# Delta stage with two inversions half a period apart, mask on VectorE, first operand space moved by 128 bytes, identity products at the stage's beginning

## The reference, cut to what matters

```python
m = jnp.where(strict, jnp.einsum('bhncd,bhnsd->bhncs', k_beta, k) * decay, 0.0)
t_inv = lax.linalg.triangular_solve(eye + m, ...)      # inverse of a 64x64 unit lower triangle
u = t_inv @ (v * beta);  w = t_inv @ (k_beta * exp(g))
def step(state, inp):                                  # 16 chunks, one after the other
    v_new = u_i - w_i @ state
    o = (q_i * exp(g_i)) @ state + a_i @ v_new
    state = state * exp(g_last) + k_dec.T @ v_new
# window: scores + mask (0 or -1e30) ; mx = max(max(scores), sink) ; p = exp(scores - mx) ; p @ v / denom
```

## Time and profile before

| | us |
|---|---|
| median of 3 runs | 2195.47 (2194.89 to 2196.8) |
| the profiled execution: its own time | 2197.01 |
| its span, first to last instruction | 2195.2 |
| delta_and_window, first GpSimd instruction to the next stage's | 335.89 to 717.39 |
| TensorE busy / VectorE / ScalarE / GpSimd | 2104.6 / 1120.2 / 725.2 / 353.0 |

### The profile page before, as it was taken

One profiled execution on the slowest core, in us unless ns is written; L12 is line 12 of the kernel. 1 busy time (PEld: TensorE's weight loads), 2 busy tenths in 40 slices (PEclk: granted clock), 3 DMA queues, 4 the chain that ended last, 5 costly groups with the idle time before them and its releaser, 6 DMA issues. The chain is left out here.

```text
span 2195.2 us, 33712 instructions
## 1 busy us (share of the span) xinstructions
PE 2104.6 (96%) x14274; PEld 1637.5 (75%) x14290; DVE 1120.2 (51%) x1724; ACT 725.2 (33%) x1344; POOL 353.0 (16%) x291
## 2 busy tenths in 40 slices
PE   7999997899998899999998999999999999999998
PEld 6888885567676687887775667778888888878877
DVE  6773335766756666563533664464433443442443
ACT  4113313333344334132314773452212212221221
POOL 3000003321322543021210323430000000000000
PEclk9999997999989899999999999999999999999999
DMA  6112322000000847712123103211111111111112
GB/s 217 48 48 86 96 87 92 1 2 2 2 2 2 302 139 275 266 40 58 59 78 150 52 17 135 77 58 48 39 58 48 38 57 51 43 39 53 49 34 101
DMA packets 186890, 167.40 MB, mean 76 GB/s; under 512 B 13472, under 2 KB 163828, under 8 KB 186100
## 3 DMA queue, kind: packets, MB, share of 16 engines
q1 hardware_dynamic: 180974, 146.75, 21.1%
q0 software_dynamic: 4784, 17.83, 2.1%
q10 hardware_dynamic: 982, 0.65, 0.1%
HBM read 138.48 MB, written 26.74 MB: 75 GB/s over the span
## 5 line engine op out<-in xcount | busy, mean ns | idle before, releaser
L250 PE MATMUL mix_acc<-mix_hi,w_hi 128*128 128x512 f32 x1040 | 415.0, 399 | 0.0
L252 PE MATMUL mix_acc<-mix_hi,w_lo 128*128 128x512 f32 x1040 | 409.3, 394 | 0.0
L251 PE MATMUL mix_acc<-m_lo,w_hi 128*128 128x512 f32 x1040 | 408.8, 393 | 0.0
L230 ACT ACTIVATE w_hi<-w_stage 128x1024 fp32r<-128x1024 f32 x154 | 162.6, 1056 | 463.3 <-PE mix_acc L252 247.2
L3178 DVE SCALAR_TENSOR_TENSOR hidden<-mix_acc,hidden_conv,hidden 128x1023 f32<-128x1023 f32 x88 | 112.8, 1282 | 263.5 <-ACT hidden L3127 262.0
L238 DVE TENSOR_TENSOR w_lo<-w_stage,w_hi 128x1024 fp32r<-128x1024 f32 x154 | 192.9, 1252 | 106.3 <-ACT w_hi L230 106.3
L250 PEld LDWEIGHTS mix_acc<-mix_hi,w_hi 128*128 128x128 f32 x1040 | 195.3, 188 | 52.0 <-issue 8.2
L252 PEld LDWEIGHTS mix_acc<-mix_hi,w_lo 128*128 128x128 f32 x1040 | 195.3, 188 | 45.7
L251 PEld LDWEIGHTS mix_acc<-m_lo,w_hi 128*128 128x128 f32 x1040 | 195.5, 188 | 43.4
L250 PE MATMUL acc<-h_hi,w_hi 128*128 128x512 f32 x400 | 156.8, 392 | 0.9 <-issue 0.9
L252 PE MATMUL acc<-h_hi,w_lo 128*128 128x512 f32 x400 | 155.8, 390 | 0.0
(11 more groups left out here) (365 smaller groups left out, 3644.0 us busy)
## 6 DMA issues: line engine op xcount, KB each, us to landing
w_stage<-in_w_in SPq DMA_DIRECT2D x48, 512.0 KB, 3.9
w_stage<-in_w_up SPq DMA_DIRECT2D x44, 512.0 KB, 3.7
w_stage<-in_w_out SPq DMA_DIRECT2D x32, 512.0 KB, 4.1
w_ada<-in_w_ada SPq DMA_DIRECT2D x32, 512.0 KB, 5.1
spill<-y_tok POOLq DMA_DIRECT2D x21, 512.0 KB, 5.1
m_resid<-resid_spill SPq DMA_DIRECT2D x2, 4096.0 KB, 16.9
conv_in<-in_w_ada SPq DMA_DIRECT2D x16, 512.0 KB, 5.6
w_stage<-in_w_down SPq DMA_DIRECT2D x16, 384.0 KB, 3.3
```

The lines of the kernel that those rows point to most:

```text
L230: nc.scalar.activation(w_hi[:, slot], w_stage[:, slot], ACT.Copy).then_inc(w_hi_ready, 1)
L250: nc.tensor.matmul(acc[:, h, :], w_hi[:, slot, k, :], hi[:, k, tok], start=k == 0, stop=False)
L251: nc.tensor.matmul(acc[:, h, :], w_hi[:, slot, k, :], lo[:, k, tok], start=False, stop=False)
L252: mm = nc.tensor.matmul(acc[:, h, :], w_lo[:, slot, k, :], hi[:, k, tok], start=False, stop=k == kts - 1)
```

## The change

1. The inversions of two steps run at once, half a period apart. A period has ten slots; the inversion of step s does levels 1 and 2 in period s (slots 1, 3, 5, 7) and levels 3 to 5 in period s+1 (slots 0, 2, 4, 6, 8, 9). The state part of step n is done in period n+2. There are 18 periods instead of 17. `tri` gets two banks; `kb` and `vb` become one bank, `value_bank`; the decays use `kvb1`. `pair_keys` gets 4 buffers, `inv` 3, `v_rest` and `v_new` one each.
2. Slot 0 carries no attention step, so a period has nine of them instead of ten.
3. The window mask is no longer a product with an identity; `masked` adds it, stores the result in SBUF and takes the row minimum of the negated scores, in one VectorE operation per head. The mask is float32 (192 KB instead of 96 KB loaded). The exponential reads SBUF.
4. The 56 identity products inside the stage go. Twenty are put about its beginning: 10 at project1's end, 5 after `gram(0)`, 5 in period 0.
5. `mix2_start` is allocated first, so that the four mix2 tensors lie 128 bytes lower.

```diff
-BF16_GROUPS = ("base16", "late", "swa")
+BF16_GROUPS = ("base16", "late")
...
                     if c == 25:
                         turn_rows()
+                keep_busy(row_bank[:, :], 10)
...
-        GAPS = [(0, 0), (0, 1), (1, 0), (1, 1), (2, 1), (3, 0), (3, 1), (4, 1), (5, 0), (5, 1)]
+        CHAIN = (("corner", 1, 3), ("corner", 0, 1), ("inverse", 1, 3), ("inverse", 0, 1), ("corner", 1, 4), ("corner", 0, 2),
+                 ("inverse", 1, 4), ("inverse", 0, 2), ("corner", 1, 5), ("inverse", 1, 5))
+        SLOTS, PERIODS = len(CHAIN), NCH + 2
...
+        window_slots = [g for g in range(WINDOW_FROM, PERIODS * SLOTS) if g % SLOTS]
+        STEP_AT = dict(zip(window_slots, WINDOW_STEPS))
...
                     for hd in range(2):
-                        m0 = (tiles[0] - i + 1) * P
-                        nc.tensor.matmul(scb[:, hd, 0:n], identb, swa[:, m0:m0 + n], start=True, stop=False)
-                    for hd in range(2):
                         r = rows_of(hd)
...
+                FIRST_FILL = {1: 1, 3: 3, 5: 1}
...
                 pairs(0)
                 gram(0)
-                for s in range(NCH + 1):
+                keep_busy(value_flat, 5)
+                for s in range(PERIODS):
+                    z = s - 2
+                    for k in range(SLOTS):
+                        kind, n, lv = chain_step(s, k)
+                        if kind == "corner":
+                            corner_sum(n, lv)
+                        elif kind == "inverse":
+                            inv_sum(n, lv)
+                        if k == 0 and z >= 0:
+                            state_sums(z)
+                        if k == 4 and z >= 0:
+                            v_sum(z)
+                        if k == 5 and s + 1 < NCH:
                             pairs(s + 1)
+                        if k == 7 and 0 <= z < NCH - 1:
+                            kv_sum(z)
+                        if k == 8 and z >= 0:
+                            out_sum(z)
+                        if k == 5 and z == NCH - 1:
+                            turn_reciprocals()
+                        if s == 0:
+                            keep_busy(value_flat, FIRST_FILL.get(k, 0))
+                        in_slot(s, k)
                     if s + 1 < NCH:
                         gram(s + 1)
...
-                        nc.scalar.activation(prob[:, u % 2, hd, 0:n], scb[:, hd, 0:n], ACT.Exp,
-                                             bias=max_neg[:, b, i, hd:hd + 1],
+                        part = prob[:, u % 2, hd, 0:n]
+                        nc.scalar.activation(part, part, ACT.Exp, bias=max_neg[:, b, i, hd:hd + 1], scale=-1.0,
...
-                    nc.vector.reduce_max(row_max[:, u % 2, :], scb[:, :, 0:n], AXX).then_inc(s_rm, 1)
-                    dve.wait_ge(s_rm, u + 1)
-                    nc.vector.scalar_tensor_tensor(max_neg[:, b, i, :], row_max[:, u % 2, :], -1.0, sink_neg[:, b:b + 5:4],
-                                                   ALU.mult, ALU.min).then_inc(s_nm, 1)
+                    for hd in range(2):
+                        nc.vector.tensor_tensor_reduce(
+                            prob[:, u % 2, hd, 0:n], scb[:, hd, 0:n], swa[:, m0:m0 + n], -1.0,
+                            sink_neg[:, b + 4 * hd:b + 4 * hd + 1], ALU.add, ALU.min,
+                            accum_out=max_neg[:, b, i, hd:hd + 1]).then_inc(s_nm if hd else s_rm, 1)
...
+                        if k == 0 and z >= 0:
+                            subtract_state(z)
+                        if k == 7 and 0 <= z < NCH - 1:
+                            advance(z, 0)
+                        if k == 8 and 0 <= z < NCH - 1:
+                            out_add(z)
+                        if k == 9 and 0 <= z < NCH - 1:
+                            advance(z, 1)
+                        if k == 9 and s + 1 < NCH:
+                            scores_of(s + 1)
+                            first_inverse(s + 1)
...
         stM2 = ExitStack()
+        sb("mix2_start", [P, 32], F32, stM2, "right")
         m_hi, m_scratch = operand_space("mix2", stM2, "right")
...
         GROUPS = ((0, 0, 6), (20, 6, 5))
-        sb("mix2_start", [P, 32], F32, stM2, "right")
```

More of the change, by code:

```diff
@@ L1045, in _ @@
                 pool.wait_ge(s_state0, 2)
-                for s in range(NCH + 1):
+                v_scaled(0)
+                decayed(0)
+                for s in range(1, PERIODS):
+                    if s == 1:
+                        pool.wait_ge(s_kdec, 2)
+                        for u in range(0, 8):
+                            cos_part(u)
+                        pool.wait_ge(s_hcos, 8)
                     if s == 2:
-                        pool.wait_ge(s_o, 2)
                         for u in range(8, NN):
@@ L1051, in _ @@
                         pool.wait_ge(s_hcos, NN)
[L1052 to L1063, removed]
+                    n = s - 2
+                    if 0 <= n < NCH - 1:
+                        v_scaled(n + 1)
+                    if 0 <= n < NCH - 2:
+                        decayed(n + 1)
+                    if n >= 0:
+                        store(n)
             @block.tensor
@@ L1110, in inv_sum @@
                             r = rows_of(hf)
-                            y, t_old = corner[r, lv, h, :], inv[r, n % 2, 1, h, :]
+                            y, t_old = corner[r, lv, h, :], inv[r, n % INV_BUFS, 1, h, :]
                             kind = kind_of(n, hf) if lv == LEVELS - 1 else 1
                             first = P + (kind * DN_HEADS + h) * LOWER
-                            mm = nc.tensor.matmul(tri[r, first:first + LOWER], y if kind else t_old,
+                            mm = nc.tensor.matmul(tri[n % 2][r, first:first + LOWER], y if kind else t_old,
                                                   upper(t_old, lv) if kind else lower(y, lv), start=True, stop=True)
@@ L1244, in values, with turn_reciprocals, in_slot @@
                     mm.then_inc(s_pv, 1)
[L1246 to L1250 removed]
+                def turn_reciprocals():
+                    pe.wait_ge(s_den, 4)
+                    for i in range(TT):
+                        mm = nc.tensor.transpose(scb[0:SW_HEADS, i // 4, i % 4 * P:(i % 4 + 1) * P], rcp[:, i, :], ident)
+                    mm.then_inc(s_mod, 1)
+                def in_slot(s, k):
+                    i = s * SLOTS + k - PREP_FROM
                     if 0 <= i < NN:
@@ L1258, in in_gap @@
                         turn_window_values(i // 2 - 2)
-                    kind, u = window_step(gap)
+                    kind, u = window_step(s, k)
                     if kind == "score":
@@ new lines, in _ @@
+                keep_busy(value_flat, 5)
+                for s in range(PERIODS):
+                    z = s - 2
+                    for k in range(SLOTS):
+                        kind, n, lv = chain_step(s, k)
+                        if kind == "corner":
+                            corner_sum(n, lv)
+                        elif kind == "inverse":
+                            inv_sum(n, lv)
[4 more added lines that the diff above has]
+                        if k == 5 and s + 1 < NCH:
+                            pairs(s + 1)
+                        if k == 7 and 0 <= z < NCH - 1:
[7 more added lines that the diff above has]
+                        in_slot(s, k)
@@ L1621, in in_gap @@
                         copy_window_values((i - 5) // 2)
-                    kind, u = window_step(gap)
+                    kind, u = window_step(s, k)
                     if kind == "score":
-                        maxima(u)
+                        masked(u)
                     elif kind == "turn1":
@@ new lines, in _ @@
+                    for k in range(SLOTS):
+                        kind, n, lv = chain_step(s, k)
+                        if kind == "corner":
+                            corner_mask(n, lv)
+                        elif kind == "inverse":
+                            inv_add(n, lv)
+                        if k == 0 and z >= 0:
+                            subtract_state(z)
[8 more added lines that the diff above has]
+                            first_inverse(s + 1)
+                        if s == 0 and k == 3:
+                            split_lo(dve, C1 + 1, (C1 + 1) % 2)
+                        if (s, k) == (NCH, 7):
+                            sink_parts()
+                        if z == NCH - 1 and k == 0:
+                            denominators()
+                        if z == NCH - 1 and k == 1:
+                            reciprocals()
+                        if z == NCH - 1 and k == 9:
+                            last_out_add()
+                        in_slot(s, k)
```

286 lines of the change are left out of this document (108 added, 178 removed).

## The result

The changed kernel takes 2185.1 us (median of 6 runs, 2181.6 to 2188.3) against 2195.2 (6 runs, 2189.7 to 2196.8) for the kernel before on the same chip: ratio 0.995, 95% interval 0.9936 to 0.9963. It is faster, by 10 us instead of the 60 forecast, and lies outside the range of 2115 to 2165. The profiled execution took 2181.63 us, the fastest of the six; its span is 2179.8.

A forecast was written before the change was run, and what follows sets the result against it. TensorE, busy 96% of the span, was taken to set the pace. Delta stage 43.5 us plus address 16.5 us gave 60.0 us off the 2195.47 median: 2135.5 us (chance 0.68), range 2115 to 2165.

The forecast's parts named there:

- the address: Last stage: all mix2 tensors at multiples of 256 bytes, 2496 products at 0.2267 instead of 0.2333 us, gaining 16.5 us.
- A steady period: Delta stage, periods 3 to 15: 17.3 us TensorE floor plus 0.8 and 0.9 of waits, 19.0 us; bounds 18.0 and 21.0.
- The 0.9 us for the store: Turn of each period: a GpSimd store slows an operation of `first_inverse` on VectorE, charged once a period.
- the copy and `values`': Attention unit's hand-overs: `turn1` waits for ScalarE's copy, `values` for VectorE's; kept at 10.0 us over 13 periods, 0.8 each.
- The beginning: Periods 0 to 2: first preparation unit at 351.8, period 1 ends at 379, period 2 takes 20 and ends at 399.
- I count one, not none: Delta stage: one dip of the clock, as in period 13 before, adding 7.3 us.
- the clock falls in the delta stage: Rival, 0.09: clock stays down, a period about 31 us, 12 more; slower from six such periods, 2284 for all 13.
- The turn of a period: Slot 9 queues nearly 4 us on VectorE; `corner_sum` of slot 1 waits, masks and `subtract_state` queue behind.
- Period 16 and the tail: End of the delta stage: period 16 takes 14 us, the tail (period 17) 8.4 us as before.
- The rival without that effect: Rival, 0.10: address is not the cause of the slower last-stage products, other engines' traffic is; 2152 us.
- the engines take turns waiting: Rival, 0.13: in the delta stage late VectorE work holds up later slots, a period stays at 21.0 us; 2161.5 us.
- the twenty products: Beginning: whether the added identity products keep the clock up is worth only 1 or 2 us; otherwise 2137, inside the forecast.

The follow-up runs named there:

- experiment 9: Changed kernel with more identity products at the beginning (16 instead of 5 after the first `gram`, more in periods 0 to 2): 2171.0 us, 0.9896 of the kernel before.
- Experiment 7: The kernel before without its 56 identity products in the delta stage: 2217.9 us, 1.0090 of the kernel before.
- experiment 4: Changed kernel with five identity products ahead of `turn1` in slots 2 and 6: 2168.1 us, 0.9873 of the kernel before.
- experiment 5: Changed kernel with the same five identity products in slots 2 and 6, but behind `turn1`: 2192.5 us, 0.9980 of the kernel before.
- experiment 6: Changed kernel, no product added; `turn1` of slots 2, 3 and 6 moved behind the next slot's sum, `v_sum` sometimes a slot earlier: 2167.9 us, 0.9861.
- experiment 1: The kernel before with only `mix2_start` allocated first: 2180.1 us, 0.9938 of the kernel before.
- experiment 2: Changed kernel with `mix2_start` allocated last again, as before: 2199.9 us, 1.0019 of the kernel before.
- experiment 8: Changed kernel without its twenty identity products at the beginning: 2178.6 us, 0.9932 of the kernel before.
- experiment 3: Changed kernel with ScalarE's `q_state` moved behind the attention step of slot 1 and the decays behind that of slot 5: 2189.0 us, 0.9970.
- experiment 10: Changed kernel with the added products of both experiment 4 and experiment 9: 2159.5 us, 0.9841 of the kernel before.
- experiment 11: Changed kernel with the later `turn1` of experiment 6 and the beginning products of experiment 9: 2156.7 us, 0.9819 of the kernel before.
- experiment 12: Experiment 11 with `decay_exp` behind the attention step of slot 5 where that step is `turn0`: 2157.9 us, 0.9838 of the kernel before.

## Why the prediction was wrong

It got the address and the steady period's length right and the clock wrong. In order of its steps:

- *A steady period, 19.0 us: right in size.* The nine periods without a dip take 19.2 us on average, 17.6 of TensorE's work (forecast 17.3) and 1.6 of its waits (forecast 0.8 + 0.9). The 0.9 us for the store isn't there: from period 1 on both operations of `first_inverse` took 0.42 or 0.43 us every time, the 0.42 of an undisturbed one in the earlier trace rows; only one in period 0, at 339.65, took 1.15, beside a GpSimd operation (`v_scaled`, 338.09 to 340.51). By the Trainium skill (SBUF — State Buffer, "Who interferes with whom") such pairs exclude each other. In the later periods they didn't meet: the stores with two inputs were over 0.2 to 1.2 us before `first_inverse` began (the one at 628.75 ended at 631.36, and it began at 631.61). That the sum was right is thus in part luck. For the copy and `values`' I kept 10 us over 13 periods; the copy's alone came to 27.3, of which 16.4 are the eight `turn1` of slots 2 and 6 in periods 3, 7, 11 and 15.
- *The beginning: the loads right, the clock missed.* The first preparation product was forecast at 351.8 and came at

```profile
351.81 2.05 PE L1189 MATMUL scb<-y_tok,window_region 128*128 128x512 f32 x2
```

  but at half clock, which lasted to 362, and period 2 lost it again from 389 on, after `turn_halves` had waited 1.64 and 1.41 us for `sin_part`. Period 1 was to end at 379 and did at 380.8; period 2 took 30.2 us instead of 20, so period 3 began at 411.0 instead of 399. With both periods at full clock (experiment 9) it begins at 400.8: about 2 of the 12 us are work that I left out, and 10 are the clock.
- *"I count one, not none": the step that failed.* Four periods of thirteen dipped. They take 113.3 us, where four at 19.0 less the 1.8 of the last make 74.2 and I had added 7.3: 31.8 us short. With the 12 of the beginning and 1.4 of the other nine periods, that is the 45 us by which the stage ended late (718.7 instead of 673.9). I argued that no product stood in the period that dipped before, and that the new stream had less idle time. The first is true and doesn't bear on it; the second is false, 35.4 us in 13 periods against 26.4. Experiment 7 shows what the 56 products did: without them the kernel before has three long dips for one, and is 23 us slower. And a mean (TensorE busy 18.96 of 21.0 us) says nothing of how the rest lies. Of period 7's 5.4 idle us, 4.3 lie in two pieces. Experiments 4, 5 and 6 show this as cause: the same products help by 17 us in the empty piece and cost 7 behind it, and other work in the piece helps as much.
- *The rival "the clock falls in the delta stage" had the mechanism.* I priced a period at 12 us; the four took 28.3 us on average, 9.3 over 19.0. I let it decide from six such periods on; four and the beginning, which I hadn't priced, took the whole gain of the stage. And I gave it 0.09 for want of a look at where the new order puts its waits. The order was there to be worked out: nine slots against units of four steps, two of ScalarE's own steps in slots 0 and 5, the mask behind `first_inverse` in slot 9.
- *The turn of a period* was named as late next, but for the wrong victim. I looked for `corner_sum` of slot 1; the one that suffered was the attention unit whose mask queues in slot 9, and through ScalarE its `turn1`.
- *Period 16 and the tail*, forecast 14 and 8.4 us: 13.8 and 8.2.
- *The address, 16.5 us: right.* 15 us both ways (experiments 1 and 2), and 0.2267 us between products. The rival without that effect is out. So is "the engines take turns waiting" at 21.0 us a period, and the twenty products were indeed worth next to nothing.

What makes a dip come in one execution and not in the next stays open. Up to the end of period 2 experiments 2, 4, 5 and 6 have the instruction stream of changed; their profiled executions took 30.1, 30.2, 22.2 and 30.2 us for period 2, at a granted clock of 0.66, 0.66, 1.00 and 0.66, behind the same two waits. So the 22.2 us in experiment 8 need not be owed to the products left out there. In the same way periods 3 and 7 took 26.8 and 26.7 us in experiment 2 and 29.2 and 29.0 in changed, and the dip of period 13 made 24.4 us in experiment 1 and 28.8 in the kernel before. Changed and experiments 2 to 6 and 8 spread over 7 to 14 us between executions, experiments 9 to 12, with period 2 at full clock, over 4 to 6 (four executions each); that would fit, but isn't shown, with one profile per kernel.

The Trainium skill (TensorE: Matmul & The Clock Gate, "A second HAM failure mode: psum-queue depth-cycling") describes a kernel whose short, frequent idle times between groups of products make the clock swing. The trace agrees: in this stage the clock fell behind waits of 0.5 to 2.9 us, single ones and short ones close together. I drew on that page for its rate of products only; this section spoke against the change.

## What to carry to other kernels

Before identity products are taken out of a stream of narrow products, run the kernel without them: here they were worth 23 us and looked like padding. When an order changes, look for the largest waits on TensorE in each phase of the new order, and for short ones close together, and not only for the sum of waits. Put work of its own there first (in experiment 6 it did as much as the products of experiment 4), products only where there is none. When a step is moved, look also at who waits for its result: in experiments 3 and 12 that made new waits. And when two changes come together, time each by itself: here an allocation's place hid that the larger one cost 4 us.

## What was not expected of the hardware

- A moving operand that starts 128 bytes past a multiple of 256 costs 0.2333 us per 128x512 product instead of 0.2267, on the same weights and at the same clock; moving it changed a 2195 us kernel by 15 us, both ways.
- Five identity products (1.25 us at full clock) in each of eight places, in a wait of about 2 us or right behind it, made a difference of 24 us over the stage.
- The same stream of instructions ran period 2 at a granted clock of 0.66 in four profiled executions and of 1.00 in a fifth.
